# Modulation rows of a two-layer trunk: fewer columns in the attention laps, the output projection and the first down projection, and 32 tiles of them in the first up projection

## The reference

```
for i in range(DEPTH):                                   # DEPTH = 2
    mod = silu(c) @ mod_w[i] + mod_b[i]                  # (2048) @ (2048, 12288)
    sh_m, sc_m, g_m, sh_f, sc_f, g_f = split(mod, 6)
    h = rms_norm(x, norm_g[i, 0]) * (1 + sc_m) + sh_m
    y = fox_attention(...) if i == 0 else rwkv7_time_mix(...)
    x = x + g_m * rms_norm(y, norm_g[i, 1])
    h = rms_norm(x, norm_g[i, 2]) * (1 + sc_f) + sh_f
    u = causal_conv_width3(h @ ffn_w_in[i])              # (2048) -> (11264)
    y = (gelu(u[:5632]) * u[5632:]) @ ffn_w_out[i]
    x = x + g_f * rms_norm(y, norm_g[i, 3])
```

## The kernel before

| stage | laps | W per lap | modulation units | tiles |
|---|---|---|---|---|
| `ph_mod` | 4 | 0 | 1 of 1024 columns per lap | 32 |
| `ph_fox`, attention | 8 | 12 | 1 of 768 per lap, second ring | 48 |
| `ph_fox_out`, output projection | 2 | 16 | 1 of 1024 per lap, second ring | 16 |
| `ph_up[0]`, up projection | 22 | 8 | none | 0 |
| `ph_down[0]`, down projection | 2 | 44 | 2 of 1024 per lap, shared ring | 32 |
| `ph_chunk`, recurrence | 8 | 0 | 1 of 1024 per lap | 64 |

## Time and profile before

### The profile page before, as it was taken

How to read it: one execution, slowest core, us unless ns; L and a number is a source line. 1 busy time by engine, 2 the same in 40 slices (tenths; PEclk the granted TensorE clock), 3 DMA queues, 4 the chain that set the end, 5 groups by cost and what they waited for, 6 DMA issues and landing times.

```text
span 3190.7 us, 62108 instructions
## 1 busy us (share of the span) xinstructions
PE 2819.6 (88%) x23550; PEld 2583.4 (81%) x23550; DVE 2181.5 (68%) x2711; ACT 1475.6 (46%) x1994; POOL 151.0 (5%) x160
## 2 busy tenths in 40 slices
PE   2399999899999998976999687777789999999998
PEld 2399998788888898975888576667687888889998
DVE  6877777876766666678564599989437666665434
ACT  0143333466667633348554222322246666665333
POOL 0000000000000000000000222311000000000000
PEclk8599999899999999997999888889799999999999
DMA  8788888656666678862565445445344566665654
GB/s 298 258 284 279 286 279 282 237 180 188 190 189 186 192 248 277 285 218 79 167 202 182 145 139 171 148 133 173 100 145 152 183 186 185 188 184 175 183 172 126
DMA packets 489766, 628.00 MB, mean 197 GB/s; under 512 B 26392, under 2 KB 434824, under 8 KB 489352
## 3 DMA queue, kind: packets, MB, share of 16 engines
q1 hardware_dynamic: 485568, 622.62, 61.1%
q10 hardware_dynamic: 4040, 3.07, 0.3%
HBM read 623.50 MB, written 2.10 MB: 196 GB/s over the span
## 4 chain that ended last, share of the span: by engine, by line
PE 69%; DVE 16%; DMA 7%; issue 4%; ACT 3%; DVEq 0%; ACTq 0%; SPq 0%
PE ps L1760 26%; PE ps L1744 21%; PE ps L1763 13%; DVE macc L1148 5%; DMA raw<-in_ffn_w_out 5%; PE ps L1937 5%; DVE wlo L1127 2%; ACT whi L727 2%; PE ps L1783 1%; PE ps L1774 1%; DMA raw<-in_fox_w_in 1%; DVE nrm L1527 1%; DVE mx L1456 1%; DVE pinv L1537 1%; DVE ut L1634 1%
## 5 line engine op out<-in xcount | busy, mean ns | idle before, releaser
L1127 DVE TENSOR_TENSOR wlo<-raw,whi 128x1024 fp32r<-128x1024 f32 x792 | 964.5, 1226 | 721.4 <-ACT whi L727 720.5
L727 ACT ACTIVATE whi<-raw 128x1024 fp32r<-128x1024 f32 x792 | 832.4, 1058 | 934.4 <-PE ps L1763 306.6
L1760 PE MATMUL ps<-xs,whi 128*128 128x512 f32 x3328 | 1170.6, 398 | 18.8 <-DVE xs L1211 10.9
L1763 PE MATMUL ps<-xs,wlo 128*128 128x256 f32 x3328 | 930.6, 280 | 0.0
L1760 PEld LDWEIGHTS ps<-xs,whi 128*128 128x128 f32 x3328 | 627.4, 189 | 171.2 <-issue 11.6
L1744 PE MATMUL ps<-act,whi 128*128 128x256 f32 x3840 | 708.4, 287 | 44.3 <-DVE wlo L1127 43.8
L1744 PEld LDWEIGHTS ps<-act,whi 128*128 128x128 f32 x3840 | 608.7, 195 | 51.3 <-DVE wlo L1127 51.0
L1763 PEld LDWEIGHTS ps<-xs,wlo 128*128 128x128 f32 x3328 | 629.4, 189 | 0.0
L1744 PE MATMUL ps<-act,wlo 128*128 128x256 f32 x1920 | 548.7, 286 | 0.0
L1148 DVE SCALAR_TENSOR_TENSOR macc<-raw,cact,macc 128x1024 f32<-128x1024 f32 (+1 forms) x364 | 450.5, 1238 | 10.8 <-DMA raw<-in_mod_w 3.2
L1744 PEld LDWEIGHTS ps<-act,wlo 128*128 128x128 f32 x1920 | 374.3, 195 | 0.0
(11 more groups left out here) (242 smaller groups left out, 3116.0 us busy)
## 6 DMA issues: line engine op xcount, KB each, us to landing
raw<-in_ffn_w_in SPq DMA_DIRECT2D x352, 512.0 KB, 3.7
raw<-in_mod_w SPq DMA_DIRECT2D x288, 512.0 KB, 4.7
raw<-in_ffn_w_out SPq DMA_DIRECT2D x176, 512.0 KB, 4.5
raw<-in_fox_w_in SPq DMA_DIRECT2D x96, 512.0 KB, 5.7
raw<-in_mod_w SPq DMA_DIRECT2D x128, 384.0 KB, 4.8
raw<-in_fox_w_out SPq DMA_DIRECT2D x32, 512.0 KB, 7.1
raw<-in_rwkv_w_r SPq DMA_DIRECT2D x32, 512.0 KB, 3.7
raw<-in_rwkv_w_k SPq DMA_DIRECT2D x32, 512.0 KB, 4.3
```

The source lines that it names most:

```text
L727: sc.activation(whi[:, half, :, :].rearrange("p k n -> p (k n)"), slots[slot], ACT.Copy).then_inc(w_hi, 1)
L1127: v.tensor_tensor(wlo[:, half, :, :].rearrange("p k n -> p (k n)"), slots[slot], whi[:, half, :, :].rearrange("p k n -> p (k n)").bitcast( ...
L1760: pe.matmul(ps[bank + m][:, :], whi[:, half, k, m * P:m * P + P], src[:, kt, :, :].rearrange("p u s -> p (u s)"), start=kt == 0, stop=Fals ...
L1763: last = pe.matmul(ps[bank + m][:, 0:S], wlo[:, half, k, m * P:m * P + P], src[:, kt, 0, :], start=False, stop=kt == KT - 1, skip_group_ch ...
```

## The change

The 192 tiles stay 192, in other places. Attention makes 640 columns per lap (tiles 32 to 71), the output projection 512 per lap (72 to 79). The first up projection makes eight units of 512 columns: four in `ph_up[0]` (tiles 80 to 95, the last gate of layer 0) and four in a new stage `ph_up_next` (the first 16 tiles of layer 1). Such a unit is spread over a group of two laps, 16 W and 16 m pieces in the one shared ring, so these eight groups are 16 of the 22 laps; the other six (`ph_up_rest`) carry none. The first down projection makes one unit of 1024 per lap, not two. The sums of the units in the up projection are kept in `sqsum` (free there) and a new buffer `mfin_up`. The waits for the finished rows in `x_norm` and `gains` follow. The rest of the diff lets one function body serve groups of two laps and of one.

```diff
+UP_GROUP, UP_GROUPS = 2, 4
...
-    ph_up[0] = Phase(UP_ITERS, "W" * 8, early=4)
-    ph_down[0] = Phase(2, "WWWW" + spread(4 * DOWN_PIECES - 4, 2 * KT), early=4)
+    with_rows = "WWWW" + spread(UP_GROUP * 8 - 6, KT) + "WW"
+    ph_up[0] = Phase(UP_GROUPS, with_rows, early=4)
+    ph_up_next = Phase(UP_GROUPS, with_rows)
+    ph_up_rest = Phase(UP_ITERS - 2 * UP_GROUPS * UP_GROUP, "W" * 8)
+    ph_down[0] = Phase(2, "WWWW" + spread(4 * DOWN_PIECES - 4, KT), early=4)
...
-    unit_cols = {ph_mod: 1024, ph_fox: 768, ph_fox_out: 1024, ph_down[0]: 1024, ph_chunk: 1024}
-    unit_tile0 = {ph_mod: 0, ph_fox: 32, ph_fox_out: 80, ph_down[0]: MODT, ph_chunk: MODT + 32}
+    unit_cols = {ph_mod: 1024, ph_fox: 640, ph_fox_out: 512, ph_up[0]: 512, ph_up_next: 512, ph_down[0]: 1024, ph_chunk: 1024}
+    unit_tile0 = {ph_mod: 0, ph_fox: 32, ph_fox_out: 72, ph_up[0]: 80, ph_up_next: MODT, ph_down[0]: MODT + 16, ph_chunk: MODT + 32}
...
+        def sums(ph):
+
+            return (sqsum, mfin_up) if ph in (ph_up[0], ph_up_next) else (macc, mfin)
...
+        up_parts = [((ph_up[0], UP_GROUP), (ph_up_next, UP_GROUP), (ph_up_rest, 1)), ((ph_up[1], 1),)]
...
-                def body(i, first):
+                def body(i, first, ph, j, w0, rows_of):
                     hooks = {7: lambda: joined(i, 0)}
...
-                    pieces(ph, i, hooks)
+                    if rows_of:
+                        hooks[4] = lambda: adaln_out(*rows_of)
+                    pieces(ph, j, hooks, w0, 8)
...
+                def body(i, first, ph, j, w0, rows_of):
+                    paired_slab(ph, j, w0, 0, xs, ready=(lambda r_: norm[2 * n + 1]["v"].at(f"lo{r_}")) if first else None)
+                    paired_slab(ph, j, w0 + 4, 2, xs)
+                    if ph.units and w0 == 8 * (UP_GROUP - 1):
+                        adaln_sum(ph, j)
```

More of the change, by code:

```diff
@@ L508, in shift_col, with up_weight, up_laps, grouped @@
             return mod[:, k:k + 1]
+        def sums(ph):
+            return (sqsum, mfin_up) if ph in (ph_up[0], ph_up_next) else (macc, mfin)
+        def up_weight(n, i, w):
+            return i * 8 + (ph_up[n].w0 + w + 1)
+        up_parts = [((ph_up[0], UP_GROUP), (ph_up_next, UP_GROUP), (ph_up_rest, 1)), ((ph_up[1], 1),)]
+        def up_laps(engine, n, body):
+            lap0 = 0
+            for k, (ph, laps) in enumerate(up_parts[n]):
+                def grouped(j, lap0=lap0, ph=ph, laps=laps, before=up_parts[n][k - 1][0] if k else None):
+                    for t in range(laps):
+                        rows_of = None
+                        if t == 0 and ph.units and not at_start(j, 0):
+                            rows_of = ph, j - 1
+                        elif t == 0 and at_start(j, 0) and before and before.units:
+                            rows_of = before, before.iters - 1
+                        body(j * laps + (lap0 + t), at_start(j, lap0 + t), ph, j, 8 * t, rows_of)
+                grouped(0)
+                with engine.Fori(1, ph.iters) as j:
+                    grouped(j)
+                lap0 += ph.iters * laps
         def waited(engine):
@@ L591, in up_pieces, with one @@
             def up_pieces(n):
[L592 to L598, removed]
+                lap0 = 0
+                for ph, per in up_parts[n]:
+                    def one(i):
+                        stream(ph, i, lambda w: w_up[n][:, 4 * (w % 4):4 * (w % 4) + 4,
+                                                        ds(i * (per * SLAB) + ((lap0 + w // 8) * SLAB + (w // 4 % 2) * FF),
+                                                           SLAB)], 1 if ph is ph_up_next else 0, unit_tile0.get(ph, 0) % MODT)
+                    laps(ph.iters, one)
+                    lap0 += ph.iters * per
+            out_pieces(ph_fox_out, fox_w_out, 4, 0, unit_tile0[ph_fox_out])
             up_pieces(0)
-            out_pieces(ph_down[0], w_down[0], DOWN_PIECES, 1, 0)
+            out_pieces(ph_down[0], w_down[0], DOWN_PIECES, 1, unit_tile0[ph_down[0]] - MODT)
             for k in range(2):
@@ L939, in body @@
                             side(i, 0)
-                laps(UP_ITERS, body)
+                up_laps(sc, n, body)
                 taps(UP_ITERS - 1, 0, s["a1"])
@@ L1135, in adaln @@
                 u, kt = divmod(m, KT)
+                part, full = sums(ph)
                 v.wait_ge(raw_in[slot], ph.landed(i, k))
@@ L1141, in adaln @@
                         v.wait_ge(raw_done, ph.done(i, k - 1))
-                    v.tensor_scalar(macc[:, 0:cols], slots[slot][:, 0:cols], cact[:, 0:1], None,
+                    v.tensor_scalar(part[:, 0:cols], slots[slot][:, 0:cols], cact[:, 0:1], None,
                                     ALU.mult).then_inc(raw_done, 1)
@@ L1772, in adaln_sum @@
                 n = unit_cols[ph] // P
+                full = sums(ph)[1]
                 for t in range(n):
-                    last = pe.matmul(pmod[:, t:t + 1], mfin[:, t * P:t * P + P], ones[:, 0:1], start=True, stop=True,
+                    last = pe.matmul(pmod[:, t:t + 1], full[:, t * P:t * P + P], ones[:, 0:1], start=True, stop=True,
                                      skip_group_check=True)
```

42 lines of the change are left out of this document (22 added, 20 removed).

## The result

| | before | with the change |
|---|---|---|
| median | 3201.89 us (4 executions) | 3260.82 us (4 executions) |
| lowest, highest | 3192.52, 3211.12 | 3254.94, 3268.84 |
| profiled execution, its span | 3192.5, 3190.7 | 3262.8, 3260.5 |

The ratio is 1.0198 with a 95% interval of 1.0167 to 1.0228: the change makes the kernel slower, by 1.7 to 2.3%. Between the two profiled executions lie 70.3 us, between the medians 58.9; what may lie behind this difference is told with the last experiment.

The account below looks back on a forecast made before the run. The prediction took TensorE to bound most stages and the four-slot ring the first down projection. Terms -1.6, -6.6, -17.3 and +104.2 made +78.7 us on 3192.5: 3271 us, range 3212 to 3312.

Parts of the forecast that it names:

- The sum: Whole kernel: -1.6 attention, -6.6 output projection, -17.3 down projection, +104.2 up projection, together +78.7 us.
- The ring: First down projection: four shared slots, not bandwidth, set its time; with 16 m pieces per lap they cease to bind, -17.3 us.
- The walk through a group: First up projection: longest chain of waits through two laps, 6 L + 18.2 = 57.9 us (L = latency + 2.37); stage +104.2 us.
- the jumps: Up projection: six steps per group where a W piece waits for its slot, each costing latency + 2.37 us, 6.62 us.
- `gelu` loop: Up projection, W1 to W2: convolution, `gelu` waiting for it, rounding and split, 4.4 us, counted once per group.
- The latency: Up projection: a W transfer taken at 4.25 us, between 3.9 and 5.0; the skill's fit of 3.2 us was set aside.
- The sums lie in the waits: Up projection: eight sums of four tiles, 6.6 us in all, cost nothing because TensorE waits anyway.
- Attention and output projection: Narrower pieces: attention -1.6 us, only sums since TensorE is full; output projection -6.6 us.
- I take 5 of 5.9 as gone: Start of the output projection: 5 of TensorE's 5.9 us idle vanish with 512 columns; bounds 0 and 5.9.
- TensorE busy about three quarters of each group: Up projection of the changed kernel: expected sign, with groups of about 58 us.
- Rival C: Up projection: queue as slow as in the down projection, latency 5.0 us, +119 us, 3312 us; chance 0.15.
- Rival A: Up projection: the shared slots have room, TensorE stays the bound, -18.9 us, 3174 us; chance 0.10.

Follow-up runs that it names:

- the last experiment: Two single edits of the kernel before: attention at 640 columns, 3182.26 us; output projection at 512, 3199.01 us. Kernel before and 640 kernel traced again: 3205.68 and 3203.92 us.
- alone: Kernel before with 16 instead of 32 modulation pieces per lap of the first down projection, 16 tiles not computed: 3185.18 us, one execution.
- The experiment with the hooks: Changed kernel with modulation pieces done ahead of the hook of their W piece in the up projection: 3238.92 us, one execution.
- the second ring: Changed kernel with the up projection's modulation pieces in their own ring of four slots: 3179.65 us, ratio 0.9937 to the kernel before.
- half the density: Kernel before with 16 tiles moved from first down to up projection, one unit per four laps, shared ring: 3180.78 us, ratio 0.9935.

## Why the prediction was right

- **The sum.** Forecast +78.7 us on the profiled execution, measured +70.3 (medians +58.9). The 2.4 us by which the work behind the down projection differs were in no term.
- **The ring bounds the down projection, and with 16 pieces per lap it no longer does.** Held. Forecast -17.3, measured -20.5 us, alone and in the change. The step counted from layer 1's down projection (263.2 us by the earlier trace rows) and added 3.3 us of sums. TensorE's waits for the splits of this stage fell from 16.8 to 4.7 us, and the stage ended at layer 1's length (264.0 us by the same rows) without the sums showing.
- **The walk through a group.** Held in kind and in size: 57.9 forecast, 56.9 measured; stage +104.2 forecast, +100.5 measured. In the group shown above, the jumps to W5, W7 and W9 are as forecast. The first goes from m15 to W1 instead of m14 to W0, and the last two by the second `gelu` loop to W12 and W14 instead of W11 and W13. In the next group the chain goes through TensorE for 33 us. So the size of a group rests in part on walks of about equal length, and that the forecast came within 1 us is partly luck. The experiment with the hooks shows it too: I knew one chain and not its neighbours, and taking 7.8 us off it gave 2.4.
- **The latency.** 4.25 us taken, 4.26 the mean of the six on the chain, though the median of all W pieces there is 4.5. By the fit in the Trainium skill, "DMA: Bandwidth & Descriptors", "Anatomy of one DMA — SWDGE (gpsimd) path", a 512 KB transfer would take 3.2 us, an estimate from a fit for transfers that GpSimd issues, not SyncE. No W transfer on the quoted chain is below 3.55, so the trace decides for the row.
- **The sums lie in the waits.** Not tested by itself. No run leaves the sums out alone, and in the group that goes through TensorE one sum of four tiles (0.79 us) lies on the chain.
- **Attention and output projection.** The total was right (-8.2 forecast, -7.8 measured), its parts were not, and this is luck. The step that failed for the output projection is "I take 5 of 5.9 as gone": its stretch is 1 to 2 us shorter in most traces with 512 columns, about the 1.6 us of the sums. The step that failed for attention is "TensorE is full, so shorter VectorE instructions and smaller transfers buy nothing". From first to last lap attention gave 7.2 us in the changed kernel's trace (301.5 against 308.7) where 1.6 were forecast. By the table above some 5 of them belong to the narrower pieces and the rest to the granted clock. TensorE's row said 44.50 of 44.50 us busy with the clock at 0.96, and yet the laps were not at their floor.
- **"TensorE busy about three quarters of each group".** Wrong: 86% (377 of 440), with the granted clock at 0.97 and matmul spans that are modelled. The lengths of the groups are the safe reading.
- **Small slips.** A modulation piece of 512 columns takes VectorE 0.75 us and not 0.68, so its sum is 42.9 of 44.5 us instead of 41.8. Rival C subtracts 24 us where the other rivals use 25.5. Neither moves the forecast.
- **Rival A** would have been right for another kernel: with the second ring the change is faster than before. Its condition, that the ring has room, is what that experiment supplied (8.7 us faster by the stages, where the rival had 18.9).

## What to carry to other kernels

When a stage is bound by one engine and others have time to spare, look at what the new work shares with the old before counting loads: here a ring of four buffers, in which each small piece holds a place for as long as VectorE takes to come to it in order. Such a ring could be priced here from the trace alone, by the longest walk of "same slot again" and "next in order" steps. When the price is to be lowered, the second longest walk counts as well (7.8 us off one walk gave 2.4). The cure here was another ring, a small one in memory that is not yet in use, or half the density. A load sum (41.8 of 44.5 us) can fit while the order does not.

Two traces of different kernels should be compared at the same granted clock, stage by stage, before a difference of a few us is given to the change.

## What was not expected of the hardware

The same up projection, instruction for instruction, runs at one of two paces for a whole stage: 22.18 or 22.61 us per lap, with nothing waiting. Windows of 200 us in the two up projections of the kernel before:

```profile
740.00:940.00 200.00, 200.00 (x1156) 174.90 (x1155) 137.85 (x181) 136.64 (x163) 0.00 (x0) 1.00 0.62 189
...
2505.00:2705.00 200.00, 200.00 (x1134) 173.49 (x1133) 135.47 (x178) 134.12 (x161) 0.00 (x0) 1.00 0.61 187
```

And the first of them in the second trace of the same kernel:

```profile
740.00:940.00 200.00, 200.00 (x1133) 173.61 (x1133) 134.66 (x175) 134.74 (x161) 0.00 (x0) 1.00 0.61 185
```

TensorE is busy throughout and granted its full clock, and does 1156 matmuls in one window and 1134 or 1133 in the others, 2% fewer. Only TensorE is slower: in the first two windows the split on VectorE takes 1223 and 1224 ns and the rounding on ScalarE 1059 and 1060. The pace changes between stages of one execution and between traces of one program. The second layer's up projection, the same in all kernels, has laps of 22.18 us in six of the fourteen traces and of 22.61 in eight. It moves this kernel by 9.3 us per up projection. What sets it, no run here shows; differences of under 10 us between single traces of different kernels should not be read without looking at the laps.
